# Seven block products in place of eight in the up projections of two conv FFNs

## Chip, core and metric

The kernel runs on one NeuronCore of a Trainium2 chip, as one program. The metric is the device time of a launch in microseconds (us). PE is TensorE, DVE is VectorE, ACT is ScalarE, Pool is GpSimd and SP the queue that issues the weight loads.

## What is computed

Two layers of a trunk with D = 1024, S = 1024 and float32 data: layer 0 with forgetting attention, layer 1 with chunked sliding-window attention, each followed by a gated MLP with a causal depthwise convolution of width 3. The change lies in this MLP:

```python
D_FF = 2816
def _conv_ffn(h, w_up, conv_w, conv_b, w_down):
    u = h @ w_up                                   # 1024 -> 2 * 2816
    up = jnp.pad(u, ((0, 0), (CONV_W - 1, 0), (0, 0)))
    conv = conv_b + sum(conv_w[j] * up[:, j:j + S] for j in range(CONV_W))
    gate, val = jnp.split(conv, 2, axis=-1)
    return (jax.nn.silu(gate) * val) @ w_down      # 2816 -> 1024
```

Its result, scaled by a modulation vector (adaLN), is added to x. The vectors for the shared keys and values and for layer 1 come from c by matrix-vector products, which layer 0's FFN carries along.

## The kernel before

All engines are programmed by hand, with semaphores. Activations lie transposed: `H[p, k, part, s]` has the 1024 features in 8 tiles of 128 partitions, all 1024 positions, and two parts. Part 0 is the value rounded to fp32r, part 1 the rest, so that a product to nearly float32 accuracy is three fp32r matmuls (high by high, high by low, low by high), each of 128x128 weights by 128x512 moving columns.

Weights come as a stream of tiles of 128x1024 (512 KB). SP loads them into two raw slots (`w_raw`) as `w_ready` tells that a slot has been read. Pool splits each into high and low part in three slots (`w_spl`), in pieces of 256 columns (L382, L387), after PE has freed the slot (`w_used`).

A layer's FFN has 22 pairs of a gate tile and a value tile. `up_tile` (96 matmuls a pair, line L435 for all matmuls of the helper `product`) fills two PSUM banks of each. ACT makes the first tap (L1137, `tap`), DVE adds the other two (L1554, L1557), ACT applies silu (L1142), DVE multiplies (L1563, `gated`), ACT and DVE split the product into `hid` (L1149, L1567). After two pairs, `down` (L729) multiplies the previous two `hid` tiles by two weight tiles: 8 outputs m of 12 matmuls each, on banks 4 to 7 in turn, so output m waits for the residual addition of output m-2 (L1574 on DVE, counted by `dn_ev`). The order on PE is: up, up, down, up, up for each `body`. On DVE, the eight residuals of a body stand behind taps and product of its first pair. In layer 0, eight bodies carry one adaLN step of 1024 columns (L1329) behind each residual, and 16 small matmuls (L452) at the end. The first pair is computed k by k, as the modulation (L1309, L920, L923, L1313) delivers H. The last `down` stands behind the last pair at once.

## Time and profile before

| | before |
|---|---|
| median of 3 runs | 2741.2 us (2737.31 to 2741.3) |
| profiled execution: time | 2741.45 us |
| profiled execution: span from first to last instruction | 2739.6 us |
| mean granted TensorE clock | 0.952 |
| FFN of layer 0, first to last matmul | 774.4 to 1552.9 us |
| FFN of layer 1 | 1947.4 to 2710.5 us |

A group of matmuls in the timeline begins when its first is issued, and its length holds the pipelined tail of the last; the distance from one group to the next, divided by the count, is the time that a matmul costs. A mean of 0.39 us for one matmul is latency, not cost.

### The profile page before, as it was taken

Reading aid. Unit: us, or ns where it says so; the run is one execution under the profiler, and the core shown is the slowest. Engines: PE = TensorE matmul, PEld = TensorE weight load, DVE = VectorE, ACT = ScalarE, POOL = GpSimd, SP = SyncE. Lnnn points to the kernel's source line nnn. Section 1 sums busy time; section 2 is a strip of 40 time slices with the busy share of each in tenths; the row PEclk is TensorE's granted clock in tenths of the full one; section 3 lists DMA queues with packets and bytes.
Section 4 is the critical chain, followed back from the end, with each engine's and each line's share of the span. In section 5 each row is a group of like instructions: output and inputs, shape, how many; then the busy total and the mean of one; then the engine's idle time right before and its main releaser. Section 6 shows DMA issues by size and latency. Waiting matters only on the chain.

```text
span 2739.6 us, 32094 instructions
## 1 busy us (share of the span) xinstructions
PE 2503.4 (91%) x11688; PEld 2077.0 (76%) x11688; DVE 1380.4 (50%) x2163; ACT 841.4 (31%) x1389; POOL 935.9 (34%) x1652
## 2 busy tenths in 40 slices
PE   5989999998989999999999798979899999999995
PEld 3878787876868888888887587768688787877773
DVE  6585756566245555544533566762433333333334
ACT  4364645556141111111111366651411111111113
POOL 1403112120534444444444352205344443444440
PEclk8999999998999999999999899969999999999997
DMA  6221212224122222222111321133011111111111
GB/s 230 71 84 55 85 51 92 62 77 150 47 100 107 101 107 103 102 93 102 67 41 45 108 74 36 37 95 114 30 49 51 45 48 47 47 46 47 47 39 62
DMA packets 70147, 205.02 MB, mean 75 GB/s; under 512 B 5888, under 2 KB 22912, under 8 KB 69904
## 3 DMA queue, kind: packets, MB, share of 16 engines
q1 hardware_dynamic: 31808, 109.06, 11.7%
q10 hardware_dynamic: 38224, 94.33, 10.1%
q8 instruction: 83, 1.36, 0.2%
q14 instruction: 32, 0.26, 0.0%
HBM read 185.09 MB, written 16.32 MB: 74 GB/s over the span
## 4 chain that ended last, share of the span: by engine, by line
PE 79%; DVE 10%; ACT 5%; issue 3%; DMA 2%; ACTq 0%; POOL 0%; DVEq 0%; SPq 0%; POOLq 0%
PE bank L435 51%; PE bank L729 18%; DVE bank L1407 1%; PE bank L631 1%; PE bank L570 1%; PE bank L485 1%; DVE X L1574 1%; DVE PL L1433 1%; PE bank L596 1%; PE bank L606 1%; PE bank L632 1%; PE bank L633 1%; PE bank L860 1%; PE bank L459 1%; PE bank L452 1%
## 5 line engine op out<-in xcount | busy, mean ns | idle before, releaser
L435 PE MATMUL bank<-H,w_spl 128*128 128x512 f32 x6240 | 1481.3, 395 | 45.5 <-DVE H L1313 27.4
L435 PEld LDWEIGHTS bank<-H,w_spl 128*128 128x128 f32 x6240 | 1178.9, 191 | 297.4 <-issue 42.7
L380 POOL TENSOR_TENSOR pace<-one_s 128x1 f32<-128x1 f32 x182 | 40.5, 223 | 1717.3 <-PE bank L435 1041.8
L387 POOL TENSOR_TENSOR w_spl<-w_raw,w_spl 128x256 fp32r<-128x256 f32 x728 | 572.4, 818 | 15.2
L729 PE MATMUL bank<-hid,w_spl 128*128 128x512 f32 x2112 | 509.6, 402 | 52.0 <-DVE X L1574 35.8
L729 PEld LDWEIGHTS bank<-hid,w_spl 128*128 128x128 f32 x2112 | 409.7, 195 | 148.7 <-DVE X L1574 44.3
L382 POOL TENSOR_SCALAR w_spl<-w_raw 128x256 fp32r<-128x256 f32 x728 | 315.5, 462 | 0.0
L1574 DVE SCALAR_TENSOR_TENSOR X<-bank,mods,X 128x1024 f32<-128x1024 f32 x176 | 224.5, 1281 | 155.9 <-PE bank L729 155.7
L1554 DVE SCALAR_TENSOR_TENSOR cV<-bank,conv_s,cV 128x1023 f32<-128x1023 f32 x44 | 56.5, 1283 | 349.5 <-ACT cV L1137 349.5
L1149 ACT ACTIVATE hid<-cV 128x1024 fp32r<-128x1024 f32 x44 | 46.7, 1062 | 571.9 <-PE bank L729 465.3
L1554 DVE SCALAR_TENSOR_TENSOR cG<-bank,conv_s,cG 128x1023 f32<-128x1023 f32 x44 | 56.4, 1283 | 307.2 <-ACT cG L1137 307.2
L981 ACT ACTIVATE PF<-bank,negFT 128x512 f32<-128x512 f32 x192 | 111.3, 580 | 154.0 <-PE bank L609 115.1
L1137 ACT ACTIVATE cG<-bank,conv_s 128x1024 f32<-128x1024 f32 x44 | 53.1, 1208 | 321.7 <-PE bank L435 321.7
L1407 DVE CUSTOM_DVE_ANT_0 bank<-bank,negF 128x128 f32<-128x128 f32 (+1 forms) x192 | 105.3, 573 | 48.2 <-PE bank L573 29.6
L1137 ACT ACTIVATE cV<-bank,conv_s 128x1024 f32<-128x1024 f32 x44 | 53.1, 1207 | 242.4 <-PE bank L435 242.4
L1433 DVE TENSOR_TENSOR PL<-PF,PH 128x512 fp32r<-128x512 f32 x192 | 111.5, 583 | 15.1 <-ACT PH L988 13.6
L631 PE MATMUL bank<-PH,V 128*128 128x512 f32 x192 | 78.3, 408 | 40.2 <-DVE PL L1433 40.0
L901 ACT ACTIVATE sq<-X 128x1024 f32<-128x1024 f32 x40 | 42.3, 1060 | 197.9 <-DVE X L1540 153.0
L988 ACT ACTIVATE PH<-PF 128x512 fp32r<-128x512 f32 x192 | 100.8, 525 | 6.1
L1540 DVE SCALAR_TENSOR_TENSOR X<-bank,mods,X 128x1024 f32<-128x1024 f32 x16 | 20.5, 1284 | 130.7 <-PE bank L435 128.6
L1142 ACT ACTIVATE cG<-cG 128x1024 f32<-128x1024 f32 x44 | 46.7, 1061 | 123.4 <-DVE cG L1557 123.4
L631 PEld LDWEIGHTS bank<-PH,V 128*128 128x128 f32 x192 | 39.7, 207 | 52.7 <-DVE PL L1433 48.6
(152 smaller groups left out, 2623.1 us busy)
## 6 DMA issues: line engine op xcount, KB each, us to landing
w_raw<-in_w_stream SPq DMA_DIRECT2D x184, 512.0 KB, 3.3
ada_raw_f<-in_ada_w ACTq DMA_DIRECT2D x6, 4096.0 KB, 15.4
ada_raw_a<-in_ada_w ACTq DMA_DIRECT2D x32, 512.0 KB, 3.8
ada_raw<-in_ada_w SPq DMA_DIRECT2D x8, 1024.0 KB, 14.3
negF<-scratch_f ACTq DMA_DIRECT2D x16, 512.0 KB, 3.8
ada_raw_f<-in_kv_ada_w ACTq DMA_DIRECT2D x2, 4096.0 KB, 14.6
X<-in_x_t SPq DMA_DIRECT2D x4, 1024.0 KB, 10.7
X<-in_x_t ACTq DMA_DIRECT2D x4, 1024.0 KB, 8.1
```

What stands on the lines that cost most here:

```text
L382: last = pool.tensor_scalar(w_spl[:, u % SPL, 0, q:q + 256], w_raw[:, u % RAW, q:q + 256], 1.0, 1.0, ALU.mult, ALU.mult)
L387: last = pool.tensor_tensor(w_spl[:, u % SPL, 1, q:q + 256], w_raw[:, u % RAW, q:q + 256], w_spl[:, u % SPL, 0, q:q + 256].bitcast(F32), A ...
L435: last = pe.matmul(dst, stat(k, a), mov(k, b), start=(k == 0 and a + b == 0), stop=(k == KT - 1 and a == 1))
L631: pe.matmul(dst, high, PH[slot][:, 0:n], start=(kb == 0), stop=False, skip_group_check=True)
L729: last = pe.matmul(bank(4 + 2 * (m % 2) + hh), w_spl[:, (slot + s) % SPL, a, m * P:m * P + P], hid[:, s, b, hh * HALF:hh * HALF + HALF], s ...
L981: nc.scalar.activation(PF[n_task % 3][:, 0:n], bank(4 + n_task % 2, 0, n), ACT.Exp, bias=negFT[:, kb, h:h + 1]).then_inc(p_exp, 1)
L988: nc.scalar.activation(PH[n_task % 3][:, 0:n], PF[n_task % 3][:, 0:n], ACT.Copy).then_inc(p_hi, 1)
L1137: nc.scalar.activation(dst, pair(2 * gv), ACT.Identity, scale=par[:, tile, 2:3].rearrange("p a b -> p (a b)"), bias=par[:, tile, 3:4].rear ...
L1407: V_.tensor_tensor_reduce(bank(c % 2, 0, n), bank(c % 2, 0, n), negF[:, h % 2, k0:k0 + n], 1.0, NEG, ALU.add, ALU.max, mx[h % 2][:, i + 4 ...
L1433: V_.tensor_tensor(PL[n_task % 3][:, 0:n], PF[n_task % 3][:, 0:n], PH[n_task % 3][:, 0:n].bitcast(F32), ALU.subtract).then_inc(p_lo, 1)
L1554: V_.scalar_tensor_tensor(dst[:, 1:S], src[:, 0:S - 1], par[:, tile, 1:2].rearrange("p a b -> p (a b)"), dst[:, 1:S], ALU.mult, ALU.add).t ...
L1574: V_.scalar_tensor_tensor(X[:, m], pair(4 + 2 * (m % 2)), mods[:, gc + m:gc + m + 1], X[:, m], ALU.mult, ALU.add).then_inc(dn_ev, 1)
```

## The change

In 20 of the 22 pairs of each layer the up projection takes the form of seven block products (Strassen's scheme in Winograd's order). The weights of a pair are four blocks: A11 and A12 are the gate tile's k = 0..3 and 4..7, A21 and A22 those of the value tile. The right side H is four blocks too: B11 and B12 are k = 0..3 in columns 0..511 and 512..1023, B21 and B22 k = 4..7. Sums of B blocks (T1 to T4) are made once a layer by DVE and ACT (`t_sums`), into `TB`, 64 KB in place of `hid` and others. Sums of A blocks (S1 to S4) are made by Pool for every pair, on the raw tiles. Each of the seven products is 12 matmuls of 512 columns, 84 a pair in place of 96. PE accumulates several into one bank; ACT copies three partial sums, and one last, from PSUM to `sU` and `s5`, and DVE makes four additions of 512 columns in PSUM before the taps (`sum_of`). The high parts of the weight blocks move from Pool to ACT (`block_high`, nine a pair); Pool makes low parts and block sums in pieces of 256 columns. Slots are now halves of 512 columns, six in all, counted by `b_used` on PE, `b_hi` on ACT and `b_ready` on Pool.

`down` is issued in halves of four outputs, one behind each pair's seven products, the two halves of one `hid` pair behind two successive pairs. `hid` lies in the columns of H that B12 had, which no product reads after the first two pairs. cG has one buffer in place of two. The adaLN vectors are computed in 32 chunks of 256 columns: 16 loads of 128 KB by ACT's queue into four buffers, 16 DVE steps of 256 columns and two groups of small matmuls in each of pairs 3 to 18 of layer 0. The loops over bodies are unrolled. Counts of matmuls of a `down` and of the adaLN matmuls remain.

```diff
+PAIRS = FT
+NORMAL = 2
+PRODUCTS = [("A11", "B11", 3), ("A12", "B21", 0), ("S1", "T1", 1), ("S2", "T2", 3), ("S4", "B22", 1),
+            ("A22", "T4", 2), ("S3", "T3", 3)]
+T_AT = {"T1": 0, "T3": 1, "T2": 2, "T4": 3}
...
-        cV = at("cV", [P, 2, S], F32, 152)
-        ada_raw_f = at("ada_raw_f", [P, KT, 1024], F32, 160)
-        ada_acc_f = at("ada_acc_f", [P, 1024], F32, 192)
+        TB = at("TB", [P, 4, 2, 4, HALF], F32R, 128)
+        TBf = at("TBf", [P, 4, 2, 4, HALF], F32, 128)
...
+        cG = at("cG", [P, S], F32, 200)
+        sU = at("sU", [P, HALF], F32, 204)
+        s5 = at("s5", [P, HALF], F32, 206)
+        S3f = at("S3f", [P, HALF], F32, 208)
+        ada_raw_f = at("ada_raw_f", [P, 4, 256], F32, 210)
+        ada_acc_f = at("ada_acc_f", [P, 256], F32, 214)
...
+            for pos in range(3, W_TILES):
+                layer = sum(pos - RAW >= w0 for w0 in W_FFN) - 1
+                if layer >= 0 and pos - RAW < W_FFN[layer] + 3 * FT:
+                    sp.wait_ge(b_ready, BLOCKS * layer + last_block_of(pos - RAW - W_FFN[layer]) + 1)
+                    load(pos, pos, None)
+                else:
...
+                def low(b, src):
+                    pool.wait_ge(b_hi, n0 + b + 1)
+                    for q in (0, 256):
+                        last = pool.tensor_tensor(block_at(layer, b, 1, q, q + 256), src[:, q:q + 256],
+                                                  block_at(layer, b, 0, q, q + 256).bitcast(F32), ALU.subtract)
+                    last.then_inc(b_ready, 1)
...
+                for p in range(NORMAL, PAIRS):
+                    t, b, n = pair_tile(p), pair_block(p), 4 * strassen_count(layer, p)
+                    a11, a12 = raw_at(layer, t, 0), raw_at(layer, t, 1)
+                    a21, a22 = raw_at(layer, t + 1, 0), raw_at(layer, t + 1, 1)
+                    low(b, a11)
+                    low(b + 1, a12)
+                    raw(t + 1)
+                    blocks(S3f[:], a11, a21, ALU.subtract)
+                    pool.wait_ge(s_sum, n + 1)
+                    blocks(a21, a21, a22, ALU.add)
+                    pool.wait_ge(s_sum, n + 2)
+                    pool.wait_ge(b_ready, n0 + b + 2)
+                    blocks(a11, a21, a11, ALU.subtract)
+                    pool.wait_ge(s_sum, n + 3)
+                    blocks(a12, a12, a11, ALU.subtract)
+                    low(b + 2, a21)
+                    low(b + 3, a11)
+                    low(b + 4, a12)
+                    low(b + 5, a22)
+                    low(b + 6, S3f[:])
+                    for s in range(2):
+                        low(b + 7 + s, raw_at(layer, t + 2, s))
...
+                def seven(p):
+                    n = strassen_count(layer, p)
+                    pe.wait_ge(cv2, 2 * FT * layer + (2 if p == NORMAL else 2 * p))
+                    for i, (name, right, b) in enumerate(PRODUCTS):
...
+                            pe.wait_ge(u_copy, 4 * n + 1)
+                        if name == "S4":
+                            pe.wait_ge(u_copy, 4 * n + 2)
+                        if name == "S3":
+                            pe.wait_ge(u_copy, 4 * n + 3)
+                        for k in range(4):
+                            if right in T_AT:
+                                mov = lambda y: TB[:, k, y, T_AT[right], :]
+                            else:
+                                k0, h0 = 4 * (right[1] == "2"), HALF * (right[2] == "2")
+                                mov = lambda y: H[:, k0 + k, y, h0:h0 + HALF]
+                            last = three(bank(b), pair_block(p) + i, k, mov, k == 0 and name in ("A11", "A12", "S1", "A22"),
+                                         k == 3, k == 0)
+                        last.then_inc(up_ps, 1)
+                        used[0] = 1
+                        if layer == 0 and name == "A11" and p in ADA_PAIRS[1:] + [ADA_PAIRS[-1] + 1]:
+                            ada(2 * (p - ADA_PAIRS[0]) - 1, p)
+                        if layer == 0 and name == "S4" and p in ADA_PAIRS:
+                            ada(2 * (p - ADA_PAIRS[0]), p)
...
+                def down(it, half):
+                    b = half_block(it, half)
+                    pe.wait_ge(b_ready, n0 + b + 2)
+                    for m in range(4 * half, 4 * half + 4):
+                        if it == 0 and m == 0:
+                            pe.wait_ge(cv2, 2 * FT * layer + 4)
+                        elif it or m >= 2:
...
+                    act.wait_ge(b_used, n0 + b - 5)
+                    if p == NORMAL and i == 0:
+                        act.wait_ge(b_hi, n0 + 4 * NORMAL)
+                    nc.scalar.activation(block_at(layer, b, 0), src, ACT.Copy).then_inc(b_hi, 1)
...
+                def u_copy_of(p, i, dst, b, sums):
+                    act.wait_ge(up_ps, up_count(layer, p, i))
+                    if sums:
+                        act.wait_ge(c_sum, sums)
+                    nc.scalar.activation(dst[:], bank(b), ACT.Copy).then_inc(u_copy, 1)
...
+                def load_ada(j):
+                    if layer or j >= 8 * ADA_CHUNKS:
+                        return
+                    chunk, k = j // 8, j % 8
+                    w_, n = (kv_ada_w, chunk) if chunk < 8 else (ada_w[1], chunk - 8)
+                    if j >= 4:
+                        act.wait_ge(ada_step, ADA_STEPS_A + j - 3)
+                    act.dma_start(ada_raw_f[:, j % 4], w_[k * P:k * P + P, 256 * n:256 * n + 256]).then_inc(adaf_in[j % 4], 16)
...
+                    block_high(p, 4)
+                    block_high(p, 5)
+                    loads(-3, 0) if p > ADA_PAIRS[0] else None
+                    if p == NORMAL:
+                        act.wait_ge(tt_lo, 8 * layer + 8)
+                    u_copy_of(p, 0, sU, 3, n)
+                    block_high(p, 6)
+                    loads(0, 2)
+                    if p % 2 == 0:
+                        high((p - 2) // 2, 0)
+                        high((p - 2) // 2, 1)
+                    block_high(p, 7)
+                    u_copy_of(p, 2, s5, 1, None)
+                    block_high(p, 8)
+                    loads(2, 6)
+                    u_copy_of(p, 3, sU, 3, n + 1)
+                    next_high(p, 0)
+                    loads(6, 8)
+                    next_high(p, 1)
+                    act.wait_ge(c_sum, n + 2)
+                    tap(p, 0, pair(0))
+                    loads(8, 10)
+                    next_high(p, 2)
+                    u_copy_of(p, 6, sU, 3, n + 2)
+                    loads(10, 12)
+                    if p == PAIRS - 1:
+                        high(FT // 2 - 1, 0)
+                    else:
+                        next_high(p, 3)
+                    act.wait_ge(c_sum, n + 4)
+                    tap(p, 1, pair(2))
+                    silu(p)
...
+                def t_sums(kk):
+                    f = 12 * layer + 3 * kk
+                    if kk:
+                        dve.wait_ge(tt_lo, 8 * layer + 2 * kk)
+                    V_.tensor_tensor(T13[:], TBf[:, kk, 0, 1:4:2, :], TBf[:, kk, 0, 0:2, :], ALU.subtract).then_inc(tt_f, 1)
+                    dve.wait_ge(tt_f, f + 1)
+                    V_.tensor_tensor(T24[:, 0], TBf[:, kk, 0, 3, :], T13[:, 0], ALU.subtract).then_inc(tt_f, 1)
+                    dve.wait_ge(tt_f, f + 2)
+                    V_.tensor_tensor(T24[:, 1], T24[:, 0], TBf[:, kk, 0, 2, :], ALU.subtract).then_inc(tt_f, 1)
+                    for i, t in enumerate((T13, T24)):
...
+                    if p > NORMAL:
+                        half_residual(p - 1, 3)
+                    if layer == 0 and p - 1 in ADA_PAIRS:
+                        ada_mods(2 * (p - 1 - ADA_PAIRS[0]) + 1)
+                    steps(0, 2)
+                    sum_of(p, 1, 1, 0, ALU.add, sU)
+                    if p % 2 == 0:
+                        low_part((p - 2) // 2, 0)
+                        low_part((p - 2) // 2, 1)
+                    steps(2, 8)
+                    sum_of(p, 4, 3, 1, ALU.add, sU)
+                    if with_ada:
+                        ada_mods(2 * (p - ADA_PAIRS[0]))
+                    steps(8, 10)
+                    taps(p, 0, pair(0))
+                    steps(10, 12)
+                    sum_of(p, 6, 4, 3, ALU.add, s5)
+                    sum_of(p, 6, 4, 2, ALU.subtract, sU)
+                    if p == PAIRS - 1:
+                        low_part(FT // 2 - 1, 0)
+                    else:
+                        steps(12, 13)
+                    half_residual(p, 0)
+                    taps(p, 1, pair(2))
+                    half_residual(p, 1)
+                    steps(13, 14)
+                    gated(p)
+                    half_residual(p, 2)
+                    steps(14, 16)
...
+        half = lambda it, h: np.concatenate([dn[(2 * it + s) * P:(2 * it + s + 1) * P, HALF * h:HALF * h + HALF]
+                                             for s in range(2)], axis=1)
+        out = []
+        for p in range(PAIRS):
+            out += ups(p)
+            if p >= NORMAL:
+                out.append(half((p - NORMAL) // 2, p % 2))
+        return out + [half(FT // 2 - 1, 0), half(FT // 2 - 1, 1)]
```

## Rows read from the trace of the kernel before

**Rows 1.** The page, engine totals: busy us, share of the span, instructions.
```profile
PE 2503.4 (91%) x11688; PEld 2077.0 (76%) x11688; DVE 1380.4 (50%) x2163; ACT 841.4 (31%) x1389; POOL 935.9 (34%) x1652
```

**Rows 2.** The page, chain that ended last: shares of the span by engine and line.
```profile
PE 79%; DVE 10%; ACT 5%; issue 3%; DMA 2%; ACTq 0%; POOL 0%; DVEq 0%; SPq 0%; POOLq 0%
PE bank L435 51%; PE bank L729 18%; DVE bank L1407 1%; PE bank L631 1%; PE bank L570 1%; PE bank L485 1%; DVE X L1574 1%; DVE PL L1433 1%; PE bank L596 1%; PE bank L606 1%; PE bank L632 1%; PE bank L633 1%; PE bank L860 1%; PE bank L459 1%;
```

**Rows 3.** Busy time in the windows of the two FFNs, layer 0 and 1.
```profile
core 0: us, PE busy (x) PEld busy (x) DVE busy (x) ACT busy (x) POOL busy (x), PEclk, DMA share, GB/s
774.40:1552.90 778.50, 749.84 (x3296) 617.54 (x3296) 378.84 (x310) 123.24 (x109) 323.55 (x576) 0.98 0.24 86
1947.40:2710.50 763.10, 734.39 (x3168) 602.07 (x3168) 305.68 (x238) 123.22 (x109) 295.84 (x567) 0.98 0.13 43
```

**Rows 4.** Timeline of PE in layer 1: start, length, group, wait before.
```profile
2018.33 5.60 PE L729 MATMUL bank<-hid,w_spl 128*128 128x512 f32 x24
2025.71 16.66 PE L729 MATMUL bank<-hid,w_spl 128*128 128x512 f32 x72 [1.78 <-DVE X L1574]
2042.21 43.68 PE L435 MATMUL bank<-H,w_spl 128*128 128x512 f32 x192
2085.73 5.60 PE L729 MATMUL bank<-hid,w_spl 128*128 128x512 f32 x24
...
2160.52 18.20 PE L729 MATMUL bank<-hid,w_spl 128*128 128x512 f32 x72 [1.79 <-DVE X L1574]
```

**Rows 5.** PE's waits over the span: us in total, times, longest.
```profile
PE bank L729 <- DVE X L1574: 35.8, 20, 1.9
...
PE bank L729 <- issue: 16.2, 2, 8.1
...
PE bank L435 <- DVE cG L1557: 5.3, 2, 2.7
```

**Rows 6.** PE windows around a wait: busy, granted clock, DMA share, GB/s.
```profile
2156.00:2160.00 4.00, 2.73 (x13) 1.00 0.15 36
2160.00:2164.00 4.00, 3.48 (x10) 0.65 0.25 99
```

**Rows 7.** Timeline of the other engines around one such wait.
```profile
2018.82 1.21 ACT L1137 ACTIVATE cV<-bank,conv_s 128x1024 f32<-128x1024 f32 x1 [6.02 <-PE bank L435]
...
2020.56 2.82 POOL L387 TENSOR_TENSOR w_spl<-w_raw,w_spl 128x256 fp32r<-128x256 f32 x4
2021.38 1.28 DVE L1557 SCALAR_TENSOR_TENSOR cV<-bank,conv_s,cV 128x1022 f32<-128x1022 f32 x1
2022.76 1.70 DVE L1563 TENSOR_TENSOR cV<-cV,cG 128x1024 f32<-128x1024 f32 x1
```

**Rows 8.** Timeline at the last down projection of layer 1.
```profile
2685.73 1.22 DVE L1567 TENSOR_TENSOR hid<-cV,hid 128x1024 fp32r<-128x1024 f32 x1 [1.12 <-ACT hid L1149]
...
2687.05 23.57 PE L729 MATMUL bank<-hid,w_spl 128*128 128x512 f32 x96 [8.11 <-issue]
```

**Rows 9.** Timeline of layer 0 at a set of small matmuls.
```profile
1100.89 1.84 PE L452 MATMUL bank<-one_s,ada_acc_f 128*128 128x1 f32 x16
...
1104.98 4.80 POOL L387 TENSOR_TENSOR w_spl<-w_raw,w_spl 128x256 fp32r<-128x256 f32 x4
1105.48 1.32 DVE L1563 TENSOR_TENSOR cV<-cV,cG 128x1024 f32<-128x1024 f32 x1
...
1107.92 1.25 DVE L1567 TENSOR_TENSOR hid<-cV,hid 128x1024 fp32r<-128x1024 f32 x1 [1.05 <-ACT hid L1149]
```

**Rows 10.** Groups by form: count, busy us, mean ns, idle before.
```profile
L988 ACT ACTIVATE PH<-PF 128x512 fp32r<-128x512 f32 x96 | 60.7, 632 | 3.1
...
L1708 DVE TENSOR_TENSOR PTB<-bank,PTB 128x512 fp32r<-128x512 f32 x32 | 22.1, 691 | 4.8 <-ACT PTB L1243 4.0
L1243 ACT ACTIVATE PTB<-bank 128x512 fp32r<-128x512 f32 x32 | 19.1, 598 | 39.7 <-PE bank L847 39.7
```

**Rows 11.** The tile of 256-column adaLN loads: ns min, median, max.
```profile
L1329 DVE SCALAR_TENSOR_TENSOR ada_acc_a<-ada_raw_a,c_act,ada_acc_a x112: 466/480/1017, 129.7 to 665.6; 128x256 f32<-128x256 f32 x112
L949 ACTq DMA_DIRECT2D ada_raw_a<-in_ada_w x32: 369/374/456, 67.5 to 655.1; - x32
```

**Rows 12.** Timeline at the start of layer 1's FFN.
```profile
1947.36 24.67 PE L435 MATMUL bank<-H,w_spl 128*128 128x512 f32 x96 [7.31 <-DVE H L1313]
...
1962.67 1.23 DVE L1313 TENSOR_TENSOR H<-hf,H 128x1024 fp32r<-128x1024 f32 x1 [1.04 <-ACT H L923]
```

**Rows 13.** DMA issues: count, KB each, median us to landing.
```profile
w_raw<-in_w_stream SPq DMA_DIRECT2D x184, 512.0 KB, 3.3
```

More of the change, by code:

```diff
@@ L781, in _ @@
+                for p in range(NORMAL, PAIRS):
+                    it, half = (p - NORMAL) // 2, p % 2
+                    seven(p)
+                    if layer == 0 and p >= ADA_PAIRS[0]:
+                        pe.wait_ge(ada_ev, N_ADA_A + min(2 * (p - ADA_PAIRS[0]) + 1, ADA_CHUNKS))
+                    down(it, half)
+                down(FT // 2 - 1, 0)
+                down(FT // 2 - 1, 1)
+                return used[0]
             out_proj(0)
             square_sum(1, 1)
-            ffn(0)
@@ L1156, in body @@
-                def body(it, dn_need, ada):
-                    for s in range(2):
-                        ut = it * 4 + (u0 + 2 * s)
-                        j = it * 2 + s
-                        tap(s, 0, bass.ds(j, 1), ut)
-                        silu(s, ut)
-                        tap(s, 1, bass.ds(j + FT, 1), ut + 1,
-                            None if dn_need is None else it * 2 + (FT * layer + s - 1))
-                        high(s, it * 2 + (FT * layer + s), dn_need)
-                        if s == 0 and ada is not None:
-                            act.wait_ge(ada_step, ada[1])
-                            load_ada(ada[0])
```

476 lines of the change are left out of this document (288 added, 188 removed).

## Prediction

> **What bounds the kernel now.** I read the engine totals first: TensorE (PE) is busy 91%, no other engine more than 50% [rows 1], and the chain that ended last is 79% PE, half of the span at the matmul line of the projections [rows 2]. Two windows hold the two FFNs, 778.5 and 763.1 us, with PE idle for some 29 us in each [rows 3]. PE's timeline in layer 1 shows the pattern. Two pairs of tiles (288 matmuls) take from 2018.33 to 2085.73, 67.4 us, or 33.7 a pair. Up matmuls follow each other every 43.52/192 = 0.2267 us, those of the down projection every 16.50/72 = 0.229; over a pair I use 0.2275 [rows 4]. After 24 matmuls of the down projection PE stands still for 1.8 us: VectorE (DVE) is late with the first residual, since ACT's tap (2018.82), DVE's two taps and the product of 1.70 us come first [rows 7]. The table of PE's waits adds these to 35.8 us in 20 waits, beside 16.2 us in two waits ahead of each last down projection, and 5.3 us at the second pair [rows 5]. Something else follows the wait: in 11 of the 20 iterations the 72 matmuls behind it take 18.2 us, not 16.6 [rows 4], with the granted clock at 0.65 in the 4 us after it, from 1.00 before: PE had paused and then ran at 1.2 instead of 2.4 GHz for a while [rows 6]. So a wait costs PE its length and, half of the time, 1.6 us more.
>
> **The matmuls removed.** A pair's up projection falls from 96 to 84 matmuls in 20 of 22 pairs of each layer: 480 fewer, of the same form. 480 x 0.2267 = -108.8 us. Nothing else lies under them, so all of it counts if PE remains fed.
>
> **The waits that go.** The down projection is now issued in halves of 4 outputs behind every pair. A half's first two outputs (24 matmuls, 5.5 us) cover two block sums (0.69 each [rows 10]) and the first residual (1.28, as a tap of the same form [rows 7]), which now stands ahead of the value taps in DVE's order. -35.8 for the waits, -11 x 1.6 = -17.6 for the low clock behind them. The last down projection waited for the whole chain of the last pair, up to the low part that ends at 2686.95, and then its 96 matmuls took 23.6 instead of 21.9 us [rows 8]. Now a half of 48 matmuls (10.9 us) lies between; the chain takes some 11.5 us from there (two sums 1.4, a high part 1.1, tap 1.2, residuals 2.6, taps 2.6, product 1.25, high and low part 2.3, less what overlaps), 0.5 us is left at most. -16.2 - 2 x 1.7 + 2 x 0.5 = -18.6.
>
> **A pair as it will be.** PE needs 132 x 0.2275 = 30.0 us. With 0 at the first product and 2.73 us for each, A22 starts at 13.65, S3 at 16.4, the half at 19.1, its outputs 2 and 3 at 24.6 and 27.3. Pool runs 18 pieces of low parts and 8 of block sums, 26 x 0.70 = 18.3 us (four pieces took 2.82 [rows 7]). ACT makes 9 block high parts and 4 copies from PSUM, 0.63 and 0.60 us each [rows 10], and as before two taps, a silu and a high part: 12.6 us. DVE adds four sums, 2.8 us. None of these is a bound by its total. The order is what can cost. The longest chain that I find begins with the release of the slot by A22's first matmul. A release or a finished product is seen 0.5 us after the next product starts, as ACT's tap at 2018.82 shows against 2018.33 [rows 4, 7].
> ACT copies block A12 of the next pair (to 14.8). Pool makes its low part, then the sums S3 and S1: six pieces, 4.3 us (to 19.1). ACT's high part of S1 stands ahead of its last PSUM copy (to 20.4). DVE makes two sums (to 21.8), then residual 0, whose product is there at 22.3 (to 23.6). The two value taps follow (to 26.2), and residual 1 (to 27.45). PE wants that at 27.3: 0.15 us late. S2 must be summed by Pool before ACT's value tap too, at 20.6, which has a microsecond of room. That is the pair of layer 1 and of the four pairs of layer 0 that carry no adaLN work: 24 x 0.15 = +3.6. Bounds: nothing if Pool is 0.2 us quicker, and 1.5 more if each of the six pieces takes 0.95, half-way to the 1.20 (4.80 for four) that a piece takes beside two DVE operations [rows 9].
>
> **Pairs 3 to 18 of layer 0.** These carry 16 adaLN steps of 256 columns on DVE, 0.48 to 0.53 us each [rows 11], a little over 8 us in all, where before 1024-column steps lay hidden in the down projection. DVE then has some 24 us of work in 31. Steps 8 to 11 read SBUF twice, and Pool's pieces lengthen while DVE does so: 4.80 in place of 2.82 [rows 9]. In the chain I give this 1.5 us, step 12 another 0.5, less 0.4 that the second small matmul group shifts PE by: PE is late by 1.6 us at output 3 (bounds 0.5, if the steps miss Pool, and 3, if each one is stretched by a Pool piece too). 16 x 1.6 = +25.6, and for the low clock 16 x 0.5 = +8. The 128 small matmuls come in 32 groups instead of 8; switching cost about 0.14 us a time (16 take 1.84 busy [rows 9]): 24 x 0.14 = +3.5. The loads of 128 KB need ACT's queue 0.37 us each [rows 11], beside its busy engine; a step waits for the load that step minus 4 released, which has 2.6 us of room, so I price it at nothing; without that room each pair loses the difference.
>
> **Start of each FFN.** DVE adds 4 groups of sums of the right side ahead of the first taps: three operations of about 1.25 and two of 0.69 each [rows 9, 10], 5.1 us a group, 21 in all. Modulation ends 16.5 us after the first matmul (1963.9 against 1947.36 [rows 12]), so they end near 38 and the taps of pair 0 (4 x 1.28) near 44, with PE wanting the banks at 46.6. Pool's pieces lie beside the SBUF pairs and can lengthen the sums by some 6 us, to which PE would then wait 3.5. ACT, after the taps of pair 1, reaches its first PSUM copy of pair 2 near 53, where PE needs it at 55. I take 2.5 us a layer and 0.8 for the clock, +6.6, against 5.3 in both layers before: +1.3. Bounds: -5.3, and +16 if both waits come.
>
> **Weight stream.** The slot of A21 and A22 is released when Pool has the pair's last low part, 11.4 us; a load lands 3.3 us later [rows 13], 14.9, and Pool asks at 16.3. Hidden by 1.4 us, and a term of the same chain if loads take 5 us. SP's queue is in order, but the load ahead was released at 4.0. Loops are unrolled; the timeline shows no gap at an iteration's edge [rows 4], so I take nothing.
>
> **Sum.** -108.8 - 35.8 - 17.6 - 18.6 + 3.6 + 25.6 + 8 + 3.5 + 1.3 = -138.8. The profiled execution took 2741.45 us (span 2739.6), 0.25 over the median of 2741.2: 2603.
>
> DVE's taps have one input in PSUM, and the one at 2021.38 took 1.28 us beside four Pool pieces, while the product of two SBUF inputs took 1.70 [rows 7]. The Trainium skill, SBUF — State Buffer, section "Who interferes with whom", says that DVE and GpSimd hold a shared port pair one instruction at a time, and that a DVE operation with at most one SBUF input stays out of it. By it the new PSUM sums cost 0.69 each, as taken; were they locked out too, each pair would have up to 1.4 us more, 24 x 1.4 = 34 us over the pairs without adaLN work. This case's trace agrees with the rule for taps; no sum of this form beside Pool is in it.
>
> **Rivals.** (A) The chain through Pool, ACT and DVE bounds every pair, not only those with adaLN work: pieces of 0.95 us, 1.5 us a pair, and 0.8 for the clock after each wait. 40 x 2.3 = 92: 2695 us. For it: no slack in the chain by my count; against: Pool's uncontended pieces are regular at 0.70. (B) Slower than before: Pool is the bound. At 1.20 us a piece, which [rows 9] shows under two DVE operations, 26 pieces take 31.2 us, and DVE's two SBUF products of 1.25 exclude it for 2.5 more: 33.7 us a pair, as before, and with the clock 2750 to 2760. It decides from 33.3 us a pair, that is 1.1 us a piece; DVE would have to be at SBUF pairs nearly always, and in layer 1 it is not. (C) The adaLN steps miss the chain and the start is covered: the amounts taken off come to 187 us with the old starts, and some 17 of the costs remain, 2741 - 187 + 17 = 2571. (D) Seven products save no time, since DVE rather than PE sets the end: the totals of [rows 1] exclude it but for (A).
>
> **Chances.** Forecast 0.62 (2583 to 2640), A 0.22, C 0.11, B and worse 0.05. The range takes C's value and most of A: 2568 to 2685. Faster by over 0.2% (5.5 us, about what a measurement of this kernel can tell from none) 0.94, same 0.01, slower 0.05.
>
> **What will show it.** 480 matmuls fewer, at the same 0.227 us spacing; two pairs of layer 1 in 60.0 to 60.5 us and of layer 0, with adaLN steps, in some 66; PE waiting mostly for the residual, and only where adaLN steps run; the granted clock near 1.00 through layer 1; Pool's pieces at 0.70 outside the steps. Wrong if layer 1's pairs take over 61.5, if PE waits for Pool's low parts or ACT's PSUM copies in the steady state, or if the clock falls in layer 1.

## The result

The changed kernel takes 2565.97 us (median of 4 runs, 2563.79 to 2568.46) where the kernel before, timed beside it, takes 2739.26 (4 runs, 2737.29 to 2741.3). The ratio is 0.9368, 95% interval 0.9351 to 0.9384. The profiled execution took 2563.79 us (span 2562.0) against 2741.45: 177.7 us less, where the prediction's sum had 138.8. The forecast was 2603, the range 2568 to 2685: the kernel is 2 us faster than the low end. Rival C ("the adaLN steps miss the chain and the start is covered", 2571) comes nearest in time. Neither of its two conditions holds fully, as shown below.

The page of the changed kernel, engine totals and then the chain that ended last:
```profile
PE 2371.5 (93%) x11208; PEld 1968.7 (77%) x11208; DVE 1583.9 (62%) x2579; ACT 1150.2 (45%) x1933; POOL 1133.5 (44%) x1568
...
PE 68%; DVE 16%; ACT 7%; DMA 4%; issue 4%; POOL 1%; ACTq 1%; DVEq 0%; SPq 0%; POOLq 0%
```
Against [rows 1] PE has 480 instructions fewer, and every other engine that computes is busier, DVE and Pool by about 200 us each, ACT by 309. The chain that ended last is still mostly PE, 68% of the span (before 79%, [rows 2]).

The windows of its two FFNs, layer 0 and 1, and one of layer 1 without start and end (columns as in [rows 3]: the stretch, its length, busy time of PE, PEld, DVE, ACT and POOL, then granted clock, DMA share, GB/s):
```profile
773.20:1471.80 698.60, 690.48 (x3056) 564.59 (x3056) 518.18 (x626) 278.70 (x381) 426.30 (x552) 0.99 0.32 98
1862.80:2534.50 671.70, 667.88 (x2928) 550.50 (x2928) 371.43 (x338) 277.00 (x381) 398.52 (x534) 1.00 0.16 48
1950.00:2500.00 550.00, 550.00 (x2426) 454.95 (x2425) 276.23 (x255) 215.57 (x314) 349.86 (x477) 1.00 0.17 54
```
PE was idle 29 us in each FFN before [rows 3]; it is idle 8.1 and 3.8 now, and never within the 550 us of layer 1, at the full granted clock. From a layer's first FFN matmul to its last, up to the sum of squares behind it, layer 0 went from 781.44 to 701.30 us and layer 1 from 765.77 to 674.33: 80.1 and 91.4 off. The other 6.1 us lie in the rest of the program.

PE's waits of the changed kernel (us in total, times, longest):
```profile
PE bank L882 <- DVE X L1891: 6.1, 14, 0.9
PE bank L882 <- POOL w_spl L543: 4.6, 2, 2.3
PE bank L631 <- DVE ada_acc_f L1622: 0.7, 2, 0.4
```
The first row corresponds to the 35.8 us of [rows 5]. Twelve of the 14 waits, 4.9 us of them, lie in layer 0 and the other two at layer 1's start. The 16.2 us ahead of the last down projections and the 5.3 us at the second pair have no successor. The second row is new: at each FFN's start Pool makes one block part 2.3 us late.

PE's timeline in layer 1, for two pairs, and behind "..." the end of the layer:
```profile
2068.61 5.60 PE L882 MATMUL bank<-TB,w_spl 128*128 128x512 f32 x24
2074.05 2.88 PE L882 MATMUL bank<-H,w_spl 128*128 128x512 f32 x12
2076.77 5.60 PE L882 MATMUL bank<-TB,w_spl 128*128 128x512 f32 x24
2082.21 16.48 PE L882 MATMUL bank<-H,w_spl 128*128 128x512 f32 x72
2098.53 5.60 PE L882 MATMUL bank<-TB,w_spl 128*128 128x512 f32 x24
...
2501.50 11.29 PE L882 MATMUL bank<-H,w_spl 128*128 128x512 f32 x48
2512.62 22.00 PE L882 MATMUL bank<-TB,w_spl 128*128 128x512 f32 x96
```
From 2068.61 to 2098.53 is one pair, 29.92 us, without a wait; the last 96 matmuls start as the 48 ahead of them end, and take 22.00 us, not the 23.57 of [rows 8].

The other engines in that pair, along the chain that the prediction followed:
```profile
2077.26 0.63 ACT L1360 ACTIVATE w_spl<-w_raw 128x512 fp32r<-128x512 f32 x1 [1.89 <-PE bank L882]
2077.97 1.43 POOL L543 TENSOR_TENSOR w_spl<-w_raw,w_spl 128x256 fp32r<-128x256 f32 x2 [1.10 <-ACT w_spl L1360]
2079.36 1.44 POOL L550 TENSOR_TENSOR S3f<-w_raw 128x256 f32<-128x256 f32 x2
2080.87 4.47 POOL L550 TENSOR_TENSOR w_raw<-w_raw 128x256 f32<-128x256 f32 x6
2082.34 0.63 ACT L1360 ACTIVATE w_spl<-w_raw 128x512 fp32r<-128x512 f32 x1 [3.35 <-POOL w_raw L550]
2082.88 0.58 ACT L1375 ACTIVATE sU<-bank 128x512 f32<-128x512 f32 x1
2083.56 0.70 DVE L1884 TENSOR_TENSOR bank<-bank,s 128x512 f32<-128x512 f32 x1 [1.94 <-ACT sU L1375]
2084.16 0.69 DVE L1882 TENSOR_TENSOR bank<-sU,bank 128x512 f32<-128x512 f32 x1
2085.13 1.28 DVE L1891 SCALAR_TENSOR_TENSOR X<-bank,mods,X 128x1024 f32<-128x1024 f32 x1 [0.28 <-PE bank L882]
2088.84 1.27 DVE L1891 SCALAR_TENSOR_TENSOR X<-bank,mods,X 128x1024 f32<-128x1024 f32 x1
```
Every link is there: ACT idles 3.35 us for Pool's S1, DVE 1.94 us for ACT's copy, the sums and the residuals follow. Residual 1 ends at 2090.11. PE wants it 36 matmuls after 2082.21, at 2082.21 + 36 x 0.227 = 2090.38: 0.27 us to spare, where the prediction had it 0.15 late.

The same chain in a pair of layer 0 with adaLN steps, PE included:
```profile
932.15 0.63 ACT L1360 ACTIVATE w_spl<-w_raw 128x512 fp32r<-128x512 f32 x1 [2.35 <-PE bank L882]
932.86 1.45 POOL L543 TENSOR_TENSOR w_spl<-w_raw,w_spl 128x256 fp32r<-128x256 f32 x2 [1.55 <-ACT w_spl L1360]
935.79 4.81 POOL L550 TENSOR_TENSOR w_raw<-w_raw 128x256 f32<-128x256 f32 x6
937.54 0.64 ACT L1360 ACTIVATE w_spl<-w_raw 128x512 fp32r<-128x512 f32 x1 [3.66 <-PE bank L882]
939.37 0.69 DVE L1882 TENSOR_TENSOR bank<-sU,bank 128x512 f32<-128x512 f32 x1
939.96 0.92 DVE L1622 SCALAR_TENSOR_TENSOR ada_acc_f<-ada_raw_f,c_act,ada_acc_f 128x256 f32<-128x256 f32 x1
940.80 1.27 DVE L1891 SCALAR_TENSOR_TENSOR X<-bank,mods,X 128x1024 f32<-128x1024 f32 x1
944.50 1.27 DVE L1891 SCALAR_TENSOR_TENSOR X<-bank,mods,X 128x1024 f32<-128x1024 f32 x1
945.83 5.74 PE L882 MATMUL bank<-H,w_spl 128*128 128x512 f32 x24 [0.35 <-DVE X L1891]
```
From ACT's high part of A12 to that of S1 it is 5.39 us here and 5.08 in layer 1: the steps stretch the chain by 0.3, not by 1.5. The same holds for the other pairs: the six Pool pieces from the low part of A12 to S1 take 4.5 to 4.8 us in each of the 16, 4.62 on average, against 4.34 in layer 1. Step 12 (the row at 939.96, 0.92 us beside Pool) stands between the second sum and residual 0, and with it residual 1 is late: PE waits, booked as 0.35 us. Step 12 takes 0.91 or 0.92 us in nine of the 16 pairs, and 0.47 or 0.48 in the other seven. PE waits for a residual in all nine, and in three of the seven. The 24 matmuls behind the wait at 945.83 take 5.74 us, so the clock did not fall. The granted clock is 1.00 over all these pairs, 860 to 1460 us.

### The profile page after: what moved, and what is told of

Its sections match the earlier page's. It is cut to its first block, busy times and chain, and to the rows that moved or that the text cites. A ratio compares the mean times of both kernels' runs of the same rounds, so it can differ in the third digit from the quotient of the medians.

```text
span 2562.0 us, 31418 instructions
## 1 busy us (share of the span) xinstructions
PE 2371.5 (93%) x11208; PEld 1968.7 (77%) x11208; DVE 1583.9 (62%) x2579; ACT 1150.2 (45%) x1933; POOL 1133.5 (44%) x1568
## 4 chain that ended last, share of the span: by engine, by line
PE 68%; DVE 16%; ACT 7%; DMA 4%; issue 4%; POOL 1%; ACTq 1%; DVEq 0%; SPq 0%; POOLq 0%
PE bank L882 41%; PE bank L614 16%; DVE ada_acc_f L1622 1%; DVE bank L1700 1%; DVE X L1891 1%; PE bank L810 1%; PE bank L749 1%; PE bank L664 1%; DVE PL L1726 1%; PE bank L775 1%; PE bank L785 1%; PE bank L1064 1%; PE bank L811 1%; PE bank L812 1%; DVE ada_acc L1622 1%
## 5 line engine op out<-in xcount | busy, mean ns | idle before, releaser
L882 PE MATMUL bank<-H,w_spl 128*128 128x512 f32 x3744 | 879.4, 393 | 25.3 <-DVE H L1606 14.6
L882 PEld LDWEIGHTS bank<-H,w_spl 128*128 128x128 f32 x3744 | 704.1, 189 | 182.3 <-issue 16.2
L543 POOL TENSOR_TENSOR w_spl<-w_raw,w_spl 128x256 fp32r<-128x256 f32 x688 | 529.3, 796 | 458.5 <-ACT w_spl L1360 457.0
L614 PE MATMUL bank<-H,w_spl 128*128 128x512 f32 x2016 | 506.1, 401 | 25.2 <-DVE H L1606 11.9
L882 PE MATMUL bank<-TB,w_spl 128*128 128x512 f32 x2112 | 494.8, 390 | 0.4 <-ACT sU L1375 0.4
L614 PEld LDWEIGHTS bank<-H,w_spl 128*128 128x128 f32 x2016 | 379.0, 192 | 107.2 <-issue 18.8
L882 PEld LDWEIGHTS bank<-TB,w_spl 128*128 128x128 f32 x2112 | 395.0, 188 | 83.2 <-issue 1.2
L1360 ACT ACTIVATE w_spl<-w_raw 128x512 fp32r<-128x512 f32 x328 | 201.8, 628 | 530.8 <-PE bank L882 369.4
L1884 DVE TENSOR_TENSOR bank<-bank,sU 128x512 f32<-128x512 f32 x80 | 55.9, 699 | 269.4 <-PE bank L882 269.3
L550 POOL TENSOR_TENSOR w_raw<-w_raw 128x256 f32<-128x256 f32 x240 | 180.0, 771 | 9.4
L493 POOL TENSOR_TENSOR w_spl<-w_raw,w_spl 128x256 fp32r<-128x256 f32 x200 | 170.4, 882 | 4.2
L1622 DVE SCALAR_TENSOR_TENSOR ada_acc_f<-ada_raw_f,c_act,ada_acc_f 128x256 f32<-128x256 f32 x224 | 134.5, 601 | 34.7 <-DMA ada_raw_f<-in_ada_w 17.4
L1375 ACT ACTIVATE sU<-bank 128x512 f32<-128x512 f32 x120 | 71.0, 592 | 127.5 <-PE bank L882 98.7
L1726 DVE TENSOR_TENSOR PL<-PF,PH 128x512 fp32r<-128x512 f32 x192 | 111.5, 583 | 16.1 <-ACT PH L1194 14.7
## 6 DMA issues: line engine op xcount, KB each, us to landing
X<-in_x_t SPq DMA_DIRECT2D x4, 1024.0 KB, 10.8
```

The costliest lines, as they stand in the source:

```text
L493: last = pool.tensor_tensor(w_spl[:, u % SPL, 1, q:q + 256], w_raw[:, u % RAW, q:q + 256], w_spl[:, u % SPL, 0, q:q + 256].bitcast(F32), A ...
L543: last = pool.tensor_tensor(block_at(layer, b, 1, q, q + 256), src[:, q:q + 256], block_at(layer, b, 0, q, q + 256).bitcast(F32), ALU.subt ...
L550: last = pool.tensor_tensor(dst[:, q:q + 256], x[:, q:q + 256], y[:, q:q + 256], op)
L614: last = pe.matmul(dst, stat(k, a), mov(k, b), start=(k == 0 and a + b == 0), stop=(k == KT - 1 and a == 1))
L882: last = pe.matmul(dst, block_at(layer, b, x, k * P, k * P + P), mov(y), start=(start and x + y == 0), stop=(stop and x == 1), skip_group_ ...
L1360: nc.scalar.activation(block_at(layer, b, 0), src, ACT.Copy).then_inc(b_hi, 1)
```

## The experiments

The kernels were timed in three groups, each beside the kernel before. It took 2737.75 us (7 runs) beside the eighth product, the two other places of the residual and its own reordered form, 2740.3 (9) beside the changed kernel again, all of Pool in 512 columns, the moved step and the sums in 64, and 2738.64 (7) beside the two kernels with part of Pool in 512.

**The changed kernel again.**

> The kernel after the change once more, to stand beside the three that follow: 2564 to 2568 us.

2567.18 us (5 runs, 2565.03 to 2570.19), ratio 0.9376 [0.9363, 0.9389]. That is the base for the three kernels timed beside it. Its layer 0 takes 698.94 us in the profiled execution, against 701.30 in the first: the same kernel differs by 2.4 us there.

**An eighth product.** What do the matmuls alone bring?
```diff
-                        for k in range(4):
+                        for k in list(range(4)) * (2 if name == "A22" else 1):
```


> The kernel after the change, with the product A22 x T4 computed twice in each of the 40 pairs (the second pass starts the bank anew, so the result is the same): 96 matmuls a pair again, in the new order. Theory (PE sets the pace of every pair, a matmul costs its whole 0.227 us): +480 x 0.227 = +109 us, less about 6 us, since the extra 2.7 us behind A22's release take the chain through Pool, ACT and DVE off PE's path in the adaLN pairs: 2669 us. So some 70 us of the gain would come from the order alone. Rival (in the adaLN pairs DVE sets the pace, so the removed matmuls were worth less there): +60 to +85, 2626 to 2650.

2665.44 us (2661.96 to 2667.94), ratio 0.9732 [0.9714, 0.9750]. PE has the 480 matmuls back and the kernel loses 99.5 us, not 108.8, since the longer pair also gives the late residuals time: no wait on them is left in its table. Layer 1, which had hardly any, lost 727.09 - 674.33 = 52.8 us, against 240 x 0.2267 = 54.4. So matmuls count at nearly their full price, 0.220 us each in layer 1, and the other 72 us of the gain come without saving one.

**The first residual behind the value taps**, the order that the kernel before has.
```diff
-                    half_residual(p, 0)
                     taps(p, 1, pair(2))
+                    half_residual(p, 0)
```


> The kernel after the change, with the first residual of each half behind DVE's two value taps, as its place was before. Theory (the new place is what took the wait away): the residual ends about 2.4 us after PE wants it for output 2, in each of 40 pairs: +96 us, 2662, if the clock stays at 2.4 GHz; with the low clock behind half of the waits, as in the kernel before, 32 more: 2694. Rival (the half of 48 matmuls alone would have hidden it): 2566 to 2580.

2703.25 us (2697.55 to 2706.94), ratio 0.9863 [0.9843, 0.9882]: this order costs 137 of the 173 us that the change gained. Its PE wait, a wait on the timeline, and the windows around that (clock: third figure from the right):
```profile
PE bank L882 <- DVE X L1891: 95.5, 40, 4.2
...
2040.17 12.79 PE L882 MATMUL bank<-H,w_spl 128*128 128x512 f32 x48 [2.19 <-DVE X L1891]
...
2036.00:2040.00 4.00, 1.98 (x9) 1.31 (x7) 3.64 (x3) 1.23 (x2) 2.31 (x4) 1.00 0.00 0
2040.00:2044.00 4.00, 3.83 (x11) 3.10 (x12) 2.44 (x3) 0.00 (x0) 0.00 (x0) 0.66 0.01 4
```
40 waits of 2.4 us, and behind this one 48 matmuls take 12.8 us in place of 11.2, part of them at 1.2 GHz. The clock falls like this behind 29 of the 40 waits, not behind half of them, and the kernel takes 9 us more than the theory's upper value.

**The first residual between the two value taps.**
```diff
-                    half_residual(p, 0)
-                    taps(p, 1, pair(2))
+                    taps(p, 1, pair(2), lambda: half_residual(p, 0))
```


> The kernel after the change, with the first residual between DVE's two value taps. Theory: PE waits 1.0 us for it in each pair, +40 us, 2604 to 2606. The granted clock behind waits of 1 us is what this run is to tell: if it falls behind half of them as behind those of 1.8 us, 2630 to 2638; if such short waits leave it at 2.4 GHz, nothing more than the 40.

2609.01 us (2608.5 to 2610.47), ratio 0.9527 [0.9511, 0.9543]: 43 more than the changed kernel. Again as many waits, each shorter:
```profile
PE bank L882 <- DVE X L1893: 41.6, 40, 2.8
...
2023.21 11.18 PE L882 MATMUL bank<-H,w_spl 128*128 128x512 f32 x48 [0.85 <-DVE X L1893]
...
2023.00:2027.00 4.00, 3.79 (x17) 3.14 (x18) 4.00 (x5) 0.00 (x0) 0.00 (x0) 1.00 0.01 4
```
The clock stays behind the 38 waits of up to 1.73 us and falls behind the other two (2.60 and 2.78 us). A wait costs a little more than its booked length even so: 41.6 - 6.1 = 35.5 us of waiting are added, and 43 us of time. One tap of 1.28 us between these two kernels is worth 94 us over 40 pairs, 2.4 a pair: 1.35 more waiting (95.5 - 41.6 over 40), and about 1 us of low clock. The clock falls behind 29 of the first kernel's waits and two of this one's, and 27 x 1.6 = 43 us; with 53.9 of waiting that is 97 for the 94 measured.

**The kernel before, with its residual first.** If the order is what counts, before gains by it too, with eight products.
```diff
-                        gated(s, ut, jt)
+                        if not (s == 0 and with_down):
+                            gated(s, ut, jt)
...
                                 residual(m, need, None if first_down else need - 8)
+                                if m == 0:
+                                    gated(s, ut, jt)
```


> The kernel before the change, with one thing altered: in a body with a down projection DVE does the first residual ahead of the product of gate and value, not behind it. Theory (a wait costs its length and, half of the time, 1.6 us of low clock): in layer 1 the wait of 1.8 us falls to 0.1 to 0.3, 10 x (1.6 + 0.8) = -24; in layer 0 with its adaLN steps a wait of about 1 us appears at output 3 instead, -10 to -18 in all: 2697 to 2706. Rival (the order is worth nothing without the halves): 2735 to 2740.

2693.12 us (2690.88 to 2694.46), ratio 0.9834 [0.9818, 0.9851]: 44.6 us off, 4 us beyond the fast end of what was expected. Its row `PE bank L729 <- DVE X L1574: 3.7, 17, 0.2` stands where [rows 5] has 35.8. The terms of the prediction for these waits and the clock behind them, -35.8 and -17.6, are thereby measured on their own: 44.6 us of their 53.4, with 3.7 us of wait left.

**Pool in pieces of 512 columns**, the part of the change that the prediction priced only in passing.
```diff
-                    for q in (0, 256):
-                        last = pool.tensor_tensor(block_at(layer, b, 1, q, q + 256), src[:, q:q + 256],
-                                                  block_at(layer, b, 0, q, q + 256).bitcast(F32), ALU.subtract)
+                    last = pool.tensor_tensor(block_at(layer, b, 1), src, block_at(layer, b, 0).bitcast(F32), ALU.subtract)
```
and the same for the sums in `blocks`.

> The kernel after the change, with Pool's block sums and low parts in single instructions of 512 columns. By the theory that PE sets the pace and Pool is off the path but for some 0.3 us: layer 1 unchanged; Pool's share falls by 0.1 to 0.2 us for each piece saved, some 2 us a pair, while DVE's adaLN steps and its product of gate and value can wait up to 1.4 us for one Pool instruction, not 0.7. Layer 0 between -6 and +8: 2560 to 2574. Rival (the size of the pieces is what keeps DVE's chain short): +15 or more, all in pairs with adaLN steps.

2610.67 us (2602.09 to 2613.65), ratio 0.9533 [0.9517, 0.9548]: 43.5 more than the changed kernel, as the rival had it, though Pool has less to do (a low part 1.34 us on average, against twice 0.80). All of it lies in layer 0, which takes 741.16 us in place of 701.30; layer 1 takes 674.49, as with pieces of 256. The new wait, and the lines around one of its occurrences:
```profile
PE bank L628 <- DVE ada_acc_f L1619: 24.5, 8, 3.1
...
959.03 3.27 DVE L1619 SCALAR_TENSOR_TENSOR ada_acc_f<-ada_raw_f,c_act,ada_acc_f 128x256 f32<-128x256 f32 x4
964.38 1.71 DVE L1619 SCALAR_TENSOR_TENSOR ada_acc_f<-ada_raw_f,c_act,ada_acc_f 128x256 f32<-128x256 f32 x2 [2.08 <-DMA ada_raw_f<-in_kv_ada_w]
966.24 0.99 PE L628 MATMUL bank<-one_s,ada_acc_f 128*128 128x1 f32 x4 [3.07 <-DVE ada_acc_f L1619]
967.09 8.42 PE L879 MATMUL bank<-TB,w_spl 128*128 128x512 f32 x24
```
Step 6 waits 2.08 us for its load, PE 3.07 us for the accumulator, and the 24 matmuls behind take 8.42 us in place of 5.75. Two causes were possible: the pieces of the down weight tile, which lie beside the early steps and so delay the loads that these release, or those ahead of S3 and S1. So each got a kernel.

**512 columns for the two low parts of the down tile alone, and for all but those.**
```diff
-                def low(b, src):
+                def low(b, src, c=256):
                     pool.wait_ge(b_hi, n0 + b + 1)
-                    for q in (0, 256):
+                    for q in range(0, 512, c):
...
-                        low(b + 7 + s, raw_at(layer, t + 2, s))
+                        low(b + 7 + s, raw_at(layer, t + 2, s), 512)
```
The second has the kernel above, with `c=512` as the default and 256 at that call.

> Of the changed kernel's 18 low-part pieces a pair, only the 4 of the two halves of the down weight tile become 2 instructions of 512 columns; the other pieces stay at 256. With all of Pool in 512 the kernel was 43.5 us slower than the changed one, and in its trace one of these two instructions (1.29 us at 958.97) holds DVE's adaLN step 2, so that the loads behind it leave 1.3 us later. Load theory: this place alone makes most of the 43.5 us, 2590 to 2612, with PE's waits at the small matmul group of the even adaLN pairs, about 3 us each in 7 or 8 of them, and a low clock behind them. Rival, the longer pieces ahead of the sums S3 and S1 are what is late: 2562 to 2572, as the changed kernel.

> The complement: all of Pool's low parts and sums in 512 columns, but the two halves of the down weight tile in pieces of 256. Load theory: the early steps run as in the changed kernel, so 2560 to 2575 with no wait over 1 us at the small matmul groups; a wait on residual 1 may be there. Rival, the pieces ahead of the sums: 2600 to 2612. If both kernels lose some 20 us the loss has two places.

The first: 2592.05 us (2586.0 to 2598.12), ratio 0.9460 [0.9438, 0.9482]. The second: 2580.82 us (2577.43 to 2584.7), ratio 0.9431 [0.9411, 0.9451]. Against 2567.7 (0.9376 x 2738.64) that is +24 and +13 us, most of the 43.5 together: the loss has two places, and the load theory has the larger. The second kernel is 6 us slower than that theory had it and 19 us faster than its rival. The waits and the steps of the first:
```profile
PE bank L631 <- DVE ada_acc_f L1622: 22.0, 8, 3.2
...
963.34 3.44 DVE L1874 TENSOR_TENSOR H<-cV,H 128x1024 fp32r<-128x1024 f32 x2
964.41 1.29 POOL L543 TENSOR_TENSOR w_spl<-w_raw,w_spl 128x512 fp32r<-128x512 f32 x1 [1.78 <-ACT w_spl L1360]
966.64 1.29 POOL L543 TENSOR_TENSOR w_spl<-w_raw,w_spl 128x512 fp32r<-128x512 f32 x1 [0.94 <-ACT w_spl L1360]
966.71 3.27 DVE L1622 SCALAR_TENSOR_TENSOR ada_acc_f<-ada_raw_f,c_act,ada_acc_f 128x256 f32<-128x256 f32 x4
968.24 2.10 ACTq L1411 DMA_DIRECT2D ada_raw_f<-in_kv_ada_w  x4
972.03 1.47 DVE L1622 SCALAR_TENSOR_TENSOR ada_acc_f<-ada_raw_f,c_act,ada_acc_f 128x256 f32<-128x256 f32 x2 [2.05 <-DMA ada_raw_f<-in_kv_ada_w]
```
and of the changed kernel at the same place of its pair:
```profile
955.44 2.89 DVE L1874 TENSOR_TENSOR H<-cV,H 128x1024 fp32r<-128x1024 f32 x2
958.26 3.90 DVE L1622 SCALAR_TENSOR_TENSOR ada_acc_f<-ada_raw_f,c_act,ada_acc_f 128x256 f32<-128x256 f32 x5
962.67 0.48 DVE L1622 SCALAR_TENSOR_TENSOR ada_acc_f<-ada_raw_f,c_act,ada_acc_f 128x256 f32<-128x256 f32 x1 [0.52 <-DMA ada_raw_f<-in_kv_ada_w]
...
959.25 2.69 ACTq L1411 DMA_DIRECT2D ada_raw_f<-in_kv_ada_w  x4
```
With long Pool pieces, DVE's low parts of two SBUF inputs take 3.44 us, not 2.89, and ACT can issue the first load that a step releases 1.53 us after the steps began, not 0.99. So the loads go out 4.9 us after the low parts began, not 3.8, step 7 ends 2.5 us later, and PE waits 2.4 to 3.2 us in each of 8 pairs. The 1.1 us at the issue become 2.5 at the step because the loads also land later. In the changed kernel the first of them is issued at 959.25 and lands 2.35 us later, ahead of a weight load that SP issues at 960.73. With long pieces it is issued at 968.24, behind the weight load of 967.96, and lands after 3.77 us: 1.1 + 1.4 = 2.5. Over the changed kernel's 256 loads of this kind the median from issue to landing is 2.2 us for the 159 issued with no weight load under way, and 4.1 for the 97 issued during one. No run moved the weight load alone. The second kernel has no such wait, but 24 waits of at most 0.7 us on residuals, 11.9 us in place of 6.1.

The Trainium skill, SBUF — State Buffer, section "Who interferes with whom", says that a DVE operation with two SBUF inputs and GpSimd hold a shared port pair one instruction at a time. The trace agrees for the steps, which read SBUF twice: the one at 966.71 takes 1.50 us beside a Pool instruction of 1.29, the three at 958.26 to 960.20 in the changed kernel 0.96, 0.78 and 0.78 beside Pool pieces half as long, and 0.48 is their time undisturbed. A sum with one input in PSUM takes 0.69 us at 963.08 beside a Pool pair.

**Step 12 behind the residuals.**
```diff
-                    else:
-                        steps(12, 13)
                     half_residual(p, 0)
...
-                    steps(13, 14)
+                    steps(12, 14)
```


> The kernel after the change, with adaLN step 12 moved from ahead of the first residual to behind the second. Theory (the 6 us of waits for a residual in layer 0 come from this step, 0.5 to 0.9 us on DVE's chain): these waits go, -5 to -7 us, 2559 to 2561. Rival (they come from Pool's sums, held up by DVE): they stay.

2556.39 us (2554.2 to 2557.11), ratio 0.9333 [0.9321, 0.9346]: 10.8 us faster than the changed kernel beside it, and the fastest here. Its waits on residuals are 3.0 us in 7 (before the move 6.1 us in 14), layer 0 takes 692.60 us, and a pair with steps 30.93. That is 29.92 and two small matmul groups of 0.50. Three of the 16 pairs with steps still wait for a residual, 0.2 to 0.3 us; it was 12 before the move (nine in the profile of the changed kernel again). So step 12 was what made residual 1 late in most of them. The 10.8 us are more than the 5 to 7 expected: against the changed kernel again, layer 0 gives 6.3 us in the profiled executions, and 3.5 lie outside the two FFNs, where nothing was altered.

**S3 and S1 in pieces of 64 columns**, 16 instructions in place of 4, to lengthen the chain through Pool alone.
```diff
-                def blocks(dst, x, y, op):
+                def blocks(dst, x, y, op, n=256):
-                    for q in (0, 256):
+                    for q in range(0, 512, n):
...
-                    blocks(S3f[:], a11, a21, ALU.subtract)
+                    blocks(S3f[:], a11, a21, ALU.subtract, 64)
-                    blocks(a21, a21, a22, ALU.add)
+                    blocks(a21, a21, a22, ALU.add, 64)
```


> The kernel after the change, with Pool's sums S3 and S1 in pieces of 64 columns in place of 256, 16 instructions in place of 4. By the fixed cost of a Pool instruction of some 0.16 us the two sums end about 2 us later, and the slack of layer 1 is 0.3 us by its timeline. Theory (the chain Pool, ACT, DVE runs close to PE's path): PE waits 1.6 to 1.8 us for the second residual in each pair, 40 x 1.7 = +68, and up to 32 more for the low clock: 2634 to 2666. Rival (the chain has room, and it was misjudged as critical): less than +20.

2632.97 us (2627.2 to 2637.85), ratio 0.9613 [0.9592, 0.9633], +65.8. Its waits, and Pool's first sum in layer 1:
```profile
PE bank L882 <- DVE X L1891: 50.1, 54, 2.0
...
2034.52 2.29 POOL L550 TENSOR_TENSOR S3f<-w_raw 128x64 f32<-128x64 f32 x8
```
S3 takes 2.29 us, not 1.44, and S1 about as much more: from ACT's high part of A12 to that of S1 it is 6.78 us, not 5.08, so 1.7 us on the chain, of which PE loses 31.36 - 29.92 = 1.4 in each pair of layer 1. The chain of rival A is real, and has some 0.3 us of room. The time lies just under the theory's range, since the clock fell behind one of these waits only.

## Why the prediction came out as it did

**What bounds, the matmuls, the waits (right).** PE is the bound. 480 x 0.2267 holds (the eighth product's layer 1: 52.8 of 54.4). The waits of 35.8 us and the low clock behind them go by order alone: the kernel before with its residual first shows it, and the two places of the residual in the changed one show the two parts. The end has gone as predicted, without the 0.5 us a layer that was kept for it. A pair of layer 1 takes 29.92 us, where 30.0 to 30.25 was forecast.

**The step that failed: pairs 3 to 18 of layer 0.** The sum has +25.6 for residual 1 being 1.6 us late, +8 for the clock, +3.5 for switching: 37.1 us. Layer 0 exceeded layer 1 by 15.7 us before and by 27.0 after, so the adaLN work costs 11.3 more than before: 25.8 of the 38.9 us missed. A pair with steps takes 31.6 us on average, where the prediction had some 33. There are three mistakes in it. First, "this 1.5 us" for Pool beside the steps: 0.3 measured. The rate of [rows 9] was taken from a place where Pool ran beside DVE products of 1.25 us, while the steps beside the six pieces are few and short; that this is the reason is argued from the timelines, and no run shows it. Step 12 was put at 0.5; it took 0.92 in nine pairs, and its move behind the residuals took away nine of the 12 waits. So it was most of what made residual 1 late. PE's waits in these pairs are 0.35 to 0.55 us, 4.9 in 12, and 0.7 in two for the accumulator. Each costs some 0.3 us more than is booked: 36 matmuls and the next start lie 8.68 us apart where one of 0.35 is booked (873.19 and 881.87), not 8.51, and behind such a wait 24 matmuls take 5.57 to 5.62 us to the next group, not 5.44. That is 14 x 0.3 = 4.2. Second, every wait was charged the half-chance of a low clock that [rows 4, 6] show behind waits of 1.8 us; behind none of these did it fall. Third, switching: 32 groups at 0.50 us are 16.0, eight at 1.84 [rows 9] 14.7, so +1.3. 4.9 + 0.7 + 4.2 + 1.3 = 11.1, and 11.3 was measured. That is closer than the parts are known. From start to start the 16 pairs take 506.20 us (859.09 to 1365.29), 27.5 more than 16 x 29.92. The groups are 16.0 of that, the waits 9.8, and 1.7 are delays too short to be booked as a wait.

**The chain itself.** Right in each link, in its order, and in being almost without room: 0.27 us early, not 0.15 late. The prediction let each finished product be seen 0.5 us after the next one starts. That is so for a released slot (ACT at 2077.26 against 2076.77), but DVE's sum starts at 2076.97, 0.2 us after. 24 x 0.15 = 3.6 became nothing.

**The load loop (wrong, and hidden by the piece size).** "Which has 2.6 us of room, so I price it at nothing": the loop has no room in the eight pairs in which DVE also makes the low parts of `hid`. In six of them the small matmul group starts 0.2 to 0.5 us late, booked as a wait in two (the third row of the changed kernel's waits), so nothing was nearly right as a price, but not for the reason given. With long pieces the loop breaks, 24 us with the down parts alone. Of the change's parts the pieces of 256 columns are worth 43.5 us, and the prediction took them for granted.

**The start (right in size).** 348 matmuls to 1948.74 take 85.93 us, 6.97 over 348 x 0.2269. Before, the first 96 and their wait had 5.55 too much. That makes +1.4 a layer, +2.9 in all, with +1.3 predicted. The largest wait there is 2.3 us for Pool's block part, which I had not named; the prediction looked for it in DVE's sums and ACT's first copy.

**The rest.** 38.9 = 25.8 (pairs 3 to 18) + 3.6 (the chain) + 1.0 (the end) - 1.6 (the start) + about 4 for the old waits, whose 24 matmuls start 7.38 us before the next ones [rows 4], so 1.94 a wait and not 1.79, and for what else lies in the FFNs, + 6.1 outside the FFNs. The "about 4" is what is left over; the old waits account for 3 of it. The 6.1 is luck as far as the runs tell: 3.3 of it lie between the two FFNs, where the kernel before took 391.5 us, the changed one 388.3, the changed one again 389.6, and the kernel before with its residual first, which differs from it in nothing there, 386.5. The kernel before alone varies by up to 12.7 us between runs of one group (2733.21 to 2745.87), so a few microseconds in such a balance can be chance.

Two slips in the prediction's arithmetic are worth 0.5 us together: 24 x 0.14 is 3.4, not 3.5, and 2741.2 - 138.8 is 2602, not 2603. And the 0.37 us of [rows 11] is ACT's queue for a load of 512 KB; one of 128 KB took 0.33.

**The chances.** C had 0.11. Its time came true, its conditions only in part: the steps do reach the chain, by 0.35 to 0.55 us in 12 pairs, and each start costs 1.4 us more than before where C had it covered. The 6.1 us outside the FFNs, which no term forecast, help to make the number fit. The bounds that I gave for the step ("0.5, if the steps miss Pool") led to it, and the range ended 2 us too high because it took C's value as its end and none of C's own spread.

## What to carry to other kernels

Where one engine is the bound and fed by another's queue, the order in that queue can be worth as much as the arithmetic saved: one tap moved was 94 us, one step of 0.9 us some 6 to 11, and one instruction moved in the kernel before took off 44.6. Size a contention term from rows of the same neighbours, not from the worst row in the trace, and look for the loop with the least room (a buffer released, a load issued, the step that waits for it) before pricing it at nothing. The size of an instruction on an engine that is nowhere near its total can decide, since another's short operation stands behind it.
